# Projection row groups reordered and a tile-by-tile start in a two-layer hybrid decoder step

## What is computed

```
h = rms_norm(x, norm1_g) @ w_in                       # (576, 1024) @ (1024, N_IN), fp32
q, k, v, qi, ki, wi, gq, gk, gv, ga, gr, gate_a, gate_b = split(h)
q, k = rope(rms_norm(q, q_g)), rope(rms_norm(k, k_g)) # per head of 64
qi, ki = rope(qi), rope(rms_norm(ki, kidx_g))         # index queries and keys
log_a = log_sigmoid(ga @ gla_wa2 + gla_ba) / 16       # decay of the linear attention (GLA)
attention over the top-k keys by sum_h wi*relu(qi.ki); GLA with decay; gates; w_oa, w_ob, w_o
x = x + merged @ w_o;  x = x + swiglu(rms_norm(x, norm2_g))
```

## Time and profile before

| | |
|---|---|
| runs | 1832.05, 1826.91, 1831.68 us; median 1831.68 |
| the profiled execution | 1833.26 us, of which 1831.5 us are its span |
| busy in the span | TensorE 1747.9, weight loads 1638.1, VectorE 1099.6, ScalarE 796.6, GpSimd 784.0 us |
| mean granted clock of TensorE | 0.988 |
| DMA | 151.06 MB, mean 82 GB/s |

### The profile page before, as it was taken

The page is one execution under the profiler, slowest core; times in us unless marked ns, Lnnn a source line. Parts: engine busy times, 40 slices in busy tenths (PEclk is TensorE's granted clock), DMA queues, the critical chain, the costliest instruction groups (busy, mean ns, idle before and its releaser), DMA issues.

```text
span 1831.5 us, 33285 instructions
## 1 busy us (share of the span) xinstructions
PE 1747.9 (95%) x12738; PEld 1638.1 (89%) x12738; DVE 1099.6 (60%) x2146; ACT 796.6 (43%) x1535; POOL 784.0 (43%) x510
## 2 busy tenths in 40 slices
PE   7998998999999999999999999999999999999998
PEld 6886897788999999999987778877899999999998
DVE  3856775365587537637647658645556874474463
ACT  4442214465566426426434332236645662363352
POOL 2323442342446447536333333515234564574452
PEclk9999999999999999999999999999999999999999
DMA  4232224214223423313222222341143234233122
GB/s 154 68 85 70 59 66 134 70 36 115 82 81 93 116 59 99 111 50 87 59 76 73 62 72 73 79 127 50 54 111 103 59 93 116 70 93 104 51 64 78
DMA packets 263303, 151.06 MB, mean 82 GB/s; under 512 B 15910, under 2 KB 255594, under 8 KB 263146
## 3 DMA queue, kind: packets, MB, share of 16 engines
q1 hardware_dynamic: 263146, 148.94, 29.5%
HBM read 141.53 MB, written 7.37 MB: 81 GB/s over the span
## 4 chain that ended last, share of the span: by engine, by line
PE 73%; DVE 14%; ACT 4%; issue 3%; SPq 3%; DMA 2%; POOL 1%; DVEq 0%; ACTq 0%; POOLq 0%
PE prod L1456 32%; PE prod L1510 8%; PE prod L1511 8%; PE prod L1512 8%; PE prod L1400 2%; PE prod L1401 2%; PE prod L1402 2%; PE aux L1867 1%; PE aux L1855 1%; SPq L1244 1%; DVE scores L2801 1%; DVE in_lo L2362 1%; SPq L1250 1%; DVE top L2799 1%; PE aux L1628 1%
## 5 line engine op out<-in xcount | busy, mean ns | idle before, releaser
L1891 POOL TENSOR_TENSOR w_lo<-w_raw,w_hi 128x1024 fp32r<-128x1024 f32 (+2 forms) x160 | 370.1, 2313 | 752.7 <-ACT w_hi L1992 748.2
L1992 ACT ACTIVATE w_hi<-w_raw 128x1024 fp32r<-128x1024 f32 (+2 forms) x160 | 163.2, 1020 | 276.4 <-PE prod L1456 244.9
L1456 PE MATMUL prod<-in_hi,w_hi 128*128 128x288 f32 x1024 | 238.8, 315 | 8.8 <-DVE in_lo L2362 7.8
L1456 PE MATMUL prod<-in_lo,w_hi 128*128 128x288 f32 x1024 | 224.4, 302 | 0.0
L1456 PE MATMUL prod<-in_hi,w_lo 128*128 128x288 f32 x1024 | 224.1, 301 | 0.0
L1510 PE MATMUL prod<-t_hi,ff_hi 128*128 128x288 f32 x704 | 208.6, 296 | 1.2 <-ACT in_sum L2046 0.6
L1456 PE MATMUL prod<-mid_hi,w_hi 128*128 128x288 f32 x960 | 207.6, 298 | 2.1 <-DVE mid_lo L2362 2.1
L1511 PE MATMUL prod<-t_lo,ff_hi 128*128 128x288 f32 x704 | 207.9, 295 | 0.0
L1512 PE MATMUL prod<-t_hi,ff_lo 128*128 128x288 f32 x704 | 207.1, 294 | 0.0
L1456 PE MATMUL prod<-mid_lo,w_hi 128*128 128x288 f32 x960 | 206.3, 296 | 0.0
L1456 PE MATMUL prod<-mid_hi,w_lo 128*128 128x288 f32 x960 | 206.3, 296 | 0.0
(11 more groups left out here) (332 smaller groups left out, 3695.7 us busy)
## 6 DMA issues: line engine op xcount, KB each, us to landing
w_raw<-in_w_in SPq DMA_DIRECT2D x72, 512.0 KB, 3.9
ff_gate<-in_w_ffn_gu SPq DMA_DIRECT2D x44, 512.0 KB, 5.2
ff_up<-in_w_ffn_gu SPq DMA_DIRECT2D x44, 512.0 KB, 4.0
w_raw<-in_w_ffn_down SPq DMA_DIRECT2D x32, 512.0 KB, 3.8
w_raw<-in_w_o SPq DMA_DIRECT2D x16, 512.0 KB, 3.9
w_raw<-in_w_ffn_down SPq DMA_DIRECT2D x16, 384.0 KB, 3.3
k_pages<-in_cache_k SPq DMA_DIRECT2D x32, 128.0 KB, 2.1
v_pages<-in_cache_v SPq DMA_DIRECT2D x32, 128.0 KB, 2.1
```

Of the source, the lines that this page charges most:

```text
L1456: ins = e.matmul(slot(g)[:, h, :], w[:, slot_w, i * P:(i + 1) * P], a[:, i, h * HALF:(h + 1) * HALF], start=first, stop=last)
L1891: e.tensor_tensor(w_lo[:, p % 2, 0:n], w_raw[:, p % RAW_RING, 0:n], w_hi[:, p % 2, 0:n].bitcast(F32), ALU.subtract).then_inc(w_lo_done, 1)
L1992: e.activation(w_hi[:, p % 2, 0:n], w_raw[:, p % RAW_RING, 0:n], ACT.Copy).then_inc(w_hi_done, 1)
```

## The change

1. The order of the row groups becomes rqi, rq, rkv (`ROW_PARTS`, `make_panels`), in both layers. The x norms and the decay chain stand in the rq panels (table `beside`), the q norms in rkv, the k norms in the gq/gk stage; qiz and the first index step move from the rgv stage to the end of the gq/gk stage, and rgv has 11 top-k rounds for 10.
2. The first layer starts tile by tile (`first_panels`): for each tile of x its transposes, ScalarE's copy (in place of VectorE's), the product with the norm weights on VectorE, in_hi on ScalarE, in_lo on VectorE, and then the matmuls of panels 0 and 1 on the tile before it. The statistics are taken afterwards, three tiles on ScalarE and two on VectorE.
3. The identity and the norm weights are loaded by ScalarE's queue; constants and small weights are loaded after panel 1 instead of before the loop; x_sample is loaded a second time to partitions 64 to 127, so that both halves of the sample rows have r_rows. ScalarE's and VectorE's steps on the sample rows now include the scale, and VectorE's separate tensor_scalar is gone.

```diff
-ROW_PARTS = {"rq": [(O_Q, ATTN_W, 0)], "rkv": [(O_K, 2 * KV_W, 0)],
-             "rqi": [(O_QI, IDX_ROW_W + IDX_HEADS, 0), (O_GA, RANK, IDX_ROW_W + IDX_HEADS)],
+ROW_PARTS = {"rqi": [(O_QI, IDX_ROW_W + IDX_HEADS, 0), (O_GA, RANK, IDX_ROW_W + IDX_HEADS)],
+             "rq": [(O_Q, ATTN_W, 0)], "rkv": [(O_K, 2 * KV_W, 0)], "rgv": [(O_GV, GV_W, 0)]}
...
-    out += rows("rq") + rows("rkv") + rows("rqi")
+    out += rows("rqi") + rows("rq") + rows("rkv")
...
+    def first_panels(self):
+
+        self.open(("gains",), 3)
+        self.add("gains")
+        self.open(("rs", "rqi"), 3)
+        self.add("panel", 0)
+        for t in range(NTILE + 1):
+            if t < NTILE:
+                self.split(("xin", t))
+                self.add("xturn", t)
+                self.add("xin", t)
+            if t < 2:
+                self.weights(t)
+            for p in range(2 if t else 0):
+                for k in range(2):
+                    self.add("unit", p, k, t - 1)
+        self.add("panel", 1)
+        self.weights(2)
+        self.add("xstat")
...
-        normed = [[("qn", part, t)] for part in ("q", "k", "x") for t in range(NTILE)]
+        normed = [[("qn", part, t)] for part in ("x", "q", "k") for t in range(NTILE)]
         self.norm_order = [step[0][1:] for step in normed]
-        for p in range(base, first["gq"]):
+        beside = {("rq", 0, 4): [("gaT",)], ("rq", 0, 6): normed[0], ("rq", 1, 2): [("z",)], ("rq", 1, 5): normed[1],
+                  ("rq", 2, 1): [("z_min",)] + normed[2], ("rq", 2, 4): [("decay",)], ("rq", 2, 6): [("decay_ref",)],
+                  ("rq", 3, 3): normed[3], ("rq", 3, 5): [("decay_exp",)], ("rq", 3, 7): normed[4]}
+        beside.update(zip([("rkv", 0, 1), ("rkv", 0, 5), ("rkv", 1, 1), ("rkv", 1, 5), ("rkv", 2, 1)], normed[NTILE:]))
...
+            if p == base + (2 if self.layer == 0 else 1):
                 self.rstd(1)
...
-        items = [[], normed[0] + [("gaT",)], [("z",)] + normed[1], [("z_min",)] + normed[2], [("decay",)],
-                 [("decay_ref",)] + normed[3],
-                 normed[4], [("qkT", 0)], [("qkT", 1), ("decay_exp",)], [("qn_end",), ("qkT", 2)], [("qkT", 3)],
-                 [("qkT", 4)]]
-        self.woven(range(first["gq"], first["rgv"]), items)
...
-        items = [[("gexp",)], [("qiz",)], [("index", 1)], [("index", 2)], topk(2), [("index", 3)], topk(2),
+        items = [[], normed[0], normed[1], normed[2], [("qkT", 0)] + normed[3], normed[4], [("qkT", 1)],
+                 [("qn_end",), ("qkT", 2)], [("qkT", 3)], [("qkT", 4)], [("qiz",)], [("index", 1)]]
+        self.woven(range(first["gq"], first["rgv"]), items)
+
+        items = [[("gexp",)] + topk(1), [("index", 2)], topk(2), [("index", 3)], topk(2),
                  [("kidx", 0)], topk(2), [("kidx", 1)], topk(2), [("sindex",)], topk(2)]
...
+            def take_x(t):
+
+                n = tile_rows(t)
+                tok = token_slice(t)
+                for half in range(2):
+                    e.wait_ge(x_turned, 2 * t + half + 1)
+                    e.activation(x_t[:, 4 * half:4 * half + 4, tok],
+                                 aux[:, 2 * (t % 2) + half, :].rearrange("p (k n) -> p k n", k=4)[:, :, 0:n],
+                                 ACT.Copy).then_inc(x_filled, 1)
+                e.wait_ge(x_gained, 2 * t + 2)
+                if t == 4:
+                    e.activation(s_both[:, :, 0:NS], x_scaled(t), ACT.Copy)
+                e.activation(in_hi[:, :, tok], x_scaled(t), ACT.Copy).then_inc(split_hi, 1)
...
+                def give_x(t):
+
+                    n = tile_rows(t)
+                    tok = token_slice(t)
+                    for half in range(2):
+                        e.wait_ge(x_filled, 2 * t + half + 1)
+                        e.tensor_tensor(x_scaled(t)[:, 4 * half:4 * half + 4, :], x_t[:, 4 * half:4 * half + 4, tok],
+                                        bcast(gains[:, 0, 4 * half:4 * half + 4], 2, n), ALU.mult).then_inc(x_gained, 1)
+                    key = ("xin", t)
+                    e.wait_ge(split_hi, split_no(key) + 1)
+                    if t == 4:
+                        e.tensor_tensor(s_both[:, :, NS:2 * NS], x_scaled(t), s_both[:, :, 0:NS].bitcast(F32),
+                                        ALU.subtract)
+                    e.tensor_tensor(in_lo[:, :, tok], x_scaled(t), in_hi[:, :, tok].bitcast(F32),
+                                    ALU.subtract).then_inc(split_lo, 1)
...
-                            e.wait_ge(free(key), emptied(key))
-                            dests = [dst for _, dst in row_dests(kind_p, 4)]
-                            if kind_p == "rq":
-                                dests = [q_rows[0:NS, 4, 0:ATTN_W]]
-                            for dst in dests:
-                                ins = e.tensor_scalar(dst, dst, r_rows[0:NS, 4:5], None, ALU.mult)
-                            ins.then_inc(rows_out[4], 1)
```

More of the change, by code:

```diff
@@ L324, in finish @@
         self.add("post", p)
-    def panel(self, p):
-        self.start(p)
-        for i in range(KD):
-            self.add("part", p, i)
-        self.finish(p)
+    def first_panels(self):
[16 more added lines that the diff above has]
+        self.add("xstat")
     def woven(self, panels, items):
@@ L465, in build_layer @@
     def build_layer(self, base):
-        if self.layer == 0:
-            self.open(("gains",), 2)
-            self.add("gains")
-            self.weights(0)
-            for kt in range(KD):
-                self.split_in(1, kt)
         first = {}
@@ L912, in build @@
         row_part_done = semaphore("row_part_done")
-        rows_out = [semaphore(f"rows{t}_out") for t in range(NTILE)]
+        rows_out = [semaphore(f"rows{t}_out") for t in range(4)]
         decay_done = semaphore("decay_done")
@@ L1038, in row_dests, with x_scaled @@
                     (lambda ps: ps[:, IDX_ROW_W:IDX_ROW_W + WGA_W], wga_rows[0:n, t, :])]
+        def x_scaled(t):
+            both = (gate_tmp, stage)[t % 2][:].rearrange("p a n -> p (a n)")
+            return both[:, 0:KD * tile_rows(t)].rearrange("p (k n) -> p k n", k=KD)
         def norm_no(norm):
@@ L1520, in body @@
                         part(step[1], step[2])
+                    elif kind == "unit":
+                        _, p, k, t = step
+                        if t == 0 and k == 0:
+                            e.wait_ge(w_lo_done, p + 1)
+                        row_unit(p, k, t)
+                    elif kind == "xturn":
+                        turn_x(step[1])
                     elif kind == "fprod":
@@ L1550, in body @@
                                                ones[:, 0:2], start=True, stop=True)
+                            ins = e.matmul(aux[NS:P, 2, 8:10], squares[:, SEQ:NT], ones[:, 0:2], start=True, stop=True)
                             ins.then_inc(ready(("rstat",)), 1)
@@ L2413, in body @@
                     kind = step[0]
+                    if kind == "xin":
+                        give_x(step[1])
+                    elif kind == "xstat":
+                        for t in (2, 3):
+                            e.wait_ge(x_loaded[t], 16)
+                            e.tensor_tensor_reduce(out=stage[:].rearrange("p a n -> p (a n)")[:, 0:D_MODEL],
+                                                   in0=x_rows[:, t, :], in1=x_rows[:, t, :], scale=1.0, scalar=0.0,
+                                                   op0=ALU.mult, op1=ALU.add,
+                                                   accum_out=r_rows[:, t:t + 1]).then_inc(x_squared_too, 1)
+                            e.wait_ge(x_squared_too, t - 1)
                     if kind == "post":
@@ L2420, in body @@
                         if kind_p in ROWS:
-                            if kind_p == "rq" and layer:
+                            if kind_p == "rqi" and layer:
                                 e.wait_ge(stored, nth(0, 16 * 3 * NTILE))
```

203 lines of the change are left out of this document (101 added, 102 removed).

## The result

| | before | after |
|---|---|---|
| median of the runs, us | 1831.86 (1826.91 to 1832.05) | 1845.37 (1843.55 to 1846.84) |
| ratio, 95% interval | | 1.0077 (1.0062 to 1.0092) |
| profiled span, us | 1831.5 | 1845.1 |

The change made the kernel slower by 0.8%. The forecast was 1821.5, so it misses by 24 us, and the result lies above the range.

What follows compares the result with a forecast made beforehand. TensorE, busy 95% of the span, was taken as the bound. Stalls removed 18.3, less start 6.1, less new lateness 2, gave 10.2 us gained: 1831.7 to 1821.5 us, own range 1815 to 1827, 8-in-10 range 1811 to 1834.

Steps and rivals of the forecast that it cites:

- The stalls that go: Row panels through gq/gk, both layers: TensorE's waits and the half clock after z vanish, gaining 18.3 us.
- What is late next: w_hi of gk's first panel and index step 2 come late: 2 us lost, range 0 to 6.4.
- Half clock: After the z matmuls: low clock disappears with the gap before z, gaining 1.5 us in first layer, 3.4 in second.
- The start costs 6.1: First layer's start: panel 2 begins 4.6 us late plus 1.5 of half clock, 6.1 us lost, bounds 1 to 10.
- The norm weights are hidden: Start: norm weights on ScalarE's queue, issued by about 2.1 us, tile 0 landing at 4.5; no cost.
- The stages from the gates on: Stages after the row panels see one topk step less and nothing waits there for it; no cost.
- w_lo beside VectorE: Start: only VectorE counted as held by GpSimd; if GpSimd is held too, up to 1 us more, making 7.1.
- ScalarE's queue: Rival, chance 0.13: w_hi of rq, k/v and gq held behind la, decay exponentials or a norm; 1850 us.
- sign of error: Forecast is wrong if panel 2 begins before 31 or after 39 us, or w_lo waits appear in rq panels.

Runs made afterwards that it cites:

- both_old_start: Changed kernel with index-key loads in two halves, decay_exp and last tile's x norm out of the last q panel, and the old start; 1822.21 us, 0.9961 of before.
- x_and_exp: Changed kernel with decay_exp and the last tile's x norm taken out of the last q panel, nothing else; 1839.09 us, 1.0066 of before.
- kidx_halves_c: Changed kernel with only the 16 cached index-key loads issued in two halves; 1838.18 us, 1.0050 of before.
- order_only_c: Changed kernel with the old start restored and the new row-group order kept; 1841.00 us, 1.0077 of before.
- turns_gains: both_turns with decay_exp in the fourth k/v panel and tile 0 turned ahead of the norm weights; 1824.22 us, 0.9954 of before.
- turn_ahead: Changed kernel with new start kept, tiles 0 to 2 turned before the first row units, 3 and 4 one unit ahead; 1.0085 of before.
- both_turns: Changed kernel with halved index-key loads, decay_exp and last x norm out of the last q panel, and tiles turned ahead; 1825.04 us, 0.9970 of before.
- both: Changed kernel with halved index-key loads and decay_exp and last tile's x norm out of the last q panel, new start kept; 1830.86 us, 1.0001 of before.

## Why the prediction was wrong

- **"The stalls that go", 18.3 us: right in kind.** Every wait named is gone: z, decay, wga_rows, wi_s, w_lo in rqi; the clock is 1.00 from 100 to 140 us. Its size was not measured alone. With both new queues relieved and the old start the new order gives 7 to 8 us. The trace of `both_old_start` says where the rest is. At the first layer's linear attention it is 3.4 us ahead of the kernel before (190.08 for 193.50): 8.4, less 2.9 because panel 2 begins at 33.21 and not 30.3 under the new order even with the old start, less the 2.4 of w_lo, is 3.1. In the second layer's row stages it gains 5.2, where 9.9 less 2.4 would be 7.5; the other 2.3 stay open. One reading was wrong as well: the wait for wga_rows is 0.5 us in the second layer too, so the term should have been 18.8.
- **"What is late next", 2 us: the step that failed.** It was bounded at 0 to 6.4 us by the longest w_lo wait of before. What stood late cost far more: x_and_exp and kidx_halves_c, which relieve one queue each, take 7.9 and 8.8 us off, 16.7 together. I looked for it at gk's w_hi and at index step 2. It was one row group and one index step away: the q rows' copies out of their banks, which I left out because I asked only what stands ahead of each w_hi, never what stands ahead of a post step that the next group's first panel needs; and index step 3, reached through SyncE's queue. Of the 16 loads I said nothing, though I wrote that the stores move; I asked what a moved step holds up on ScalarE and GpSimd, and not on SyncE.
- **Half clock.** I counted the dips that would go (4.9 us) and none that a new wait would bring. The four new waits, 14.9 us together, brought 2.9, 3.4, 3.4 and 1.7, 11.4 us.
- **"The start costs 6.1": too small, and near a measured figure by luck.** The term is reckoned against the 30.3 of the kernel before, and so panel 2 is 6.6 us late, not 4.6, and the clock costs 1.7, not 1.5: 8.3. The 6.0 of order_only_c (and 7.3 under the repairs) is another quantity, the gain from the old start under the new order, where panel 2 begins at 33.11 and is 3.8 earlier. 128x1024 on VectorE took 1.22 for my 1.2, the first row matmul came at 13.39, not 11.9, panel 2 at 36.91, not 34.9.
- **"The norm weights are hidden": wrong.** I let them be "issued by about 2.1 us" and gave no landing time. They landed at 6.01 and held tile 0's transposes by 1.4 us (6.19 against 4.81 in turns_gains). Of turns_gains's lead at the front 0.65 to 0.9 us was left at panel 2 (31.88, against 32.53 in turn_ahead and 32.78 in both_turns), and nothing that the time shows.
- **The stages from the gates on, "nothing waits there for it": wrong.** The wait for g_attn grew from 1.89 to 2.98 us in both layers. In both_old_start the clock behind it is 0.50 and 0.72 for 4 us each in the first layer and 0.62 for 4 us in the second, 4.6 us lost, where it was 1.00 before. No run takes this apart.
- **w_lo beside VectorE.** The sentence drawn from the Trainium skill, SBUF — State Buffer, "SBUF: two separate sides", let GpSimd be held as well and would have made the start 7.1. The trace agrees, in both directions. The w_lo of 11.35 took 0.34 us more than the 1.65 of the earlier trace rows, and in_lo (10.64 to 11.86) was running for its first 0.51 us; those of 16.32 and 34.74 took 0.35 and 0.47 more, beside VectorE operations that ran on for 0.52 and 0.64. The products that came after a w_lo had begun took 2.59 for two that otherwise take 1.47. My chain had only the second kind.
- **The rivals.** The one that came closest is "ScalarE's queue", at 0.13: the right engine and the wrong work behind it, since no q or k/v panel waited for its w_lo. A quarter of its price came true there, and as much again through SyncE. Neither sign of error that the forecast named came true, panel 2 outside 31 to 39 us or w_lo waits in the rq panels; the time was wrong all the same.

**The version that beats both** is the new order with both queues relieved and the old start: 0.9961 (0.9945 to 0.9977) with 12 runs, and 0.9954 and 0.9960 for its two neighbours, 1822 to 1823 us against 1830. Part of what the order was meant to bring is there. The new start adds nothing to it: repaired as well as I could (turns_gains, 0.9954), it only draws level with the old one.

## What to carry to other kernels

When a step moves, list for every engine *and* for the DMA-issuing queue what now stands ahead of the next thing that TensorE needs, including the copies that empty a bank, not only the weight conversions. A block of loads that goes out in one piece holds every weight load behind it; splitting it is one small edit and was worth 8.8 us here, and nothing in the old order. Price a long gap of TensorE at more than its length: the four of 3.6 to 3.9 us here, 14.9 in all, were followed by 11.4 lost to the clock. And reckon a new start and an old one with the same panels behind them, or the gain of one looks like the cost of the other.

## What the hardware showed that I had not expected

- Gaps of 3.6 to 4 us on TensorE were followed by 5 to 8 us at a granted clock of 0.50 to 0.77 in the changed kernel (86 to 94, 166 to 174, 993 to 1000, 1074 to 1079 us). The traces of all versions that have one of these two waits show 32 such gaps, 3.6 to 4.3 us long; behind each, 1.4 to 3.4 us are lost in the next 8 (an estimate, from the granted clock of two stretches of 4 us).
- Shorter gaps were followed by a low clock in some places and not in others. The wait of 2.4 us at the first gq panel stands in eight places of four versions: behind three of them 1.7 us are lost, behind five the clock is 1.00. Behind the 2.51 us before panel 2, `both` got 0.50 for 6 us, after three more gaps of 0.8 to 1.2 us since 25; the changed kernel, with nearly the same gaps, got 0.53 for 3 us and then 0.90.
- Sixteen loads of cached index keys kept SyncE issuing for 17.24 us, 1.08 each, while one load of rows takes 0.42 in the earlier trace rows. The record of each issue is only 0.33 us; the rest lies between the records, where SyncE reads the page number that the address needs. How the rest divides was not measured.
- VectorE and GpSimd hold each other up in either order: w_lo took 0.34, 0.35 and 0.47 us more when a VectorE operation was still running for its first 0.51, 0.52 and 0.64 us, and VectorE's 128x8 copy took 2.40 beside a w_lo of 2.40 that had begun 0.03 us earlier (76.98 and 76.95).
